# Squares, bonus input and k's scaling of a time-mixing stage on GpSimd, with other buffers and banks

## The reference

```python
w = -softplus(-(w0 + tanh(xw @ w1) @ w2)) - 0.5
decay = exp(-exp(w))
a = sigmoid(a0 + (xa @ a1) @ a2)
g = sigmoid(xg @ g1) @ g2
kk = heads(k * k_k)
kk = kk / maximum(sqrt(sum(kk * kk, -1)), 1e-12)
k = k * (1 + (a - 1) * k_a)
...
bonus = sum(rh * kh * r_k, -1) * vh
out = ((norm(y) + bonus) * g) @ w_o
```

## Time and profile before

| | |
|---|---|
| time, median of 3 runs | 3338.79 us (3338.55 to 3340.55) |
| profiled execution, its own time | 3345.62 us |
| span of that execution | 3343.8 us |
| TensorE matmul, weight load | 3082.7 us (92%), 2754.2 us (82%) |
| VectorE | 2405.0 us (72%) |
| ScalarE | 1660.4 us (50%) |
| GpSimd | 123.0 us (4%) |
| granted TensorE clock, mean | 0.933 of full |

### The profile page before, as it was taken

How to read it: one execution, slowest core, us unless ns; L and a number is a source line. 1 busy time by engine, 2 the same in 40 slices (tenths; PEclk the granted TensorE clock), 3 DMA queues, 4 the chain that set the end, 5 groups by cost and what they waited for, 6 DMA issues and landing times. The chain is left out here.

```text
span 3343.8 us, 58689 instructions
## 1 busy us (share of the span) xinstructions
PE 3082.7 (92%) x23865; PEld 2754.2 (82%) x23865; DVE 2405.0 (72%) x3656; ACT 1660.4 (50%) x2382; POOL 123.0 (4%) x178
## 2 busy tenths in 40 slices
PE   7679999899888899999988899999999998988899
PEld 6567778689877789898976899899789898878798
DVE  6569999688775468787577578786578788674555
ACT  4437777554552354544552444544554544442444
POOL 0010000000102000000000000000000001011000
PEclk8779999899999799999986899999999999998899
DMA  9347999667410267586430377674157586300442
GB/s 382 140 170 288 400 402 373 247 262 310 178 64 4 95 249 305 219 313 265 155 137 1 120 298 281 257 306 178 74 229 306 221 314 260 116 2 3 166 182 80
DMA packets 77519, 698.09 MB, mean 209 GB/s; under 512 B 8433, under 2 KB 12657, under 8 KB 55409
## 3 DMA queue, kind: packets, MB, share of 16 engines
q1 hardware_dynamic: 30928, 525.06, 39.8%
q10 hardware_dynamic: 42912, 157.31, 12.4%
q0 software_dynamic: 3456, 12.58, 1.0%
HBM read 690.72 MB, written 4.19 MB: 208 GB/s over the span
## 5 line engine op out<-in xcount | busy, mean ns | idle before, releaser
L1075 PE MATMUL banks<-u_split,w_split 128*128 128x512 f32 x2816 | 1014.7, 403 | 23.3 <-DVE u_split L1320 21.2
L1144 ACT ACTIVATE w_split<-ring 128x1024 fp32r<-128x1024 f32 x513 | 541.4, 1058 | 672.6 <-PE banks L1076 408.8
L1251 DVE TENSOR_TENSOR w_split<-ring,w_split 128x1024 fp32r<-128x1024 f32 x513 | 625.9, 1223 | 293.9 <-ACT w_split L1144 290.0
L1076 PE MATMUL banks<-u_split,w_split 128*128 128x256 f32 x2816 | 797.0, 283 | 0.0
L1075 PEld LDWEIGHTS banks<-u_split,w_split 128*128 128x128 f32 x2816 | 536.8, 191 | 159.3 <-issue 17.6
L1076 PEld LDWEIGHTS banks<-u_split,w_split 128*128 128x128 f32 x2816 | 539.6, 192 | 0.0
L1067 PE MATMUL banks<-h_split,w_split 128*128 128x256 f32 x1408 | 400.7, 285 | 7.5 <-DVE w_split L1251 7.5
L1068 PE MATMUL banks<-h_split,w_split 128*128 128x256 f32 x1408 | 400.4, 284 | 0.0
L1069 PE MATMUL banks<-h_split,w_split 128*128 128x256 f32 x1408 | 400.3, 284 | 0.0
L521 PE MATMUL banks<-bufs_split,ring_split 128*128 128x256 f32 x1376 | 397.3, 289 | 0.0
L585 DVE CUSTOM_DVE_ANT_0 bufs<-bufs 128x1024 f32<-128x1024 f32 x300 | 357.0, 1224 | 12.0 <-DVE w_split L1251 12.0
(11 more groups left out here) (497 smaller groups left out, 4872.4 us busy)
## 6 DMA issues: line engine op xcount, KB each, us to landing
ring<-stream SPq DMA_DIRECT2D x155, 3072.0 KB, 11.0
bufs<-ada ACTq DMA_DIRECT2D x296, 512.0 KB, 10.7
bufs<-ada POOLq DMA_DIRECT2D x23, 512.0 KB, 6.6
bufs<-ada SPq DMA_DIRECT2D x3, 2048.0 KB, 16.0
ring<-stream SPq DMA_DIRECT2D x2, 2688.0 KB, 9.0
bufs<-c_rows SPq DMA_DIRECT2D x9, 512.0 KB, 4.4
ring<-stream SPq DMA_DIRECT2D x1, 2704.0 KB, 13.1
ring<-stream SPq DMA_DIRECT2D x1, 2176.0 KB, 8.4
```

The source lines that it names most:

```text
L1075: pe.matmul(bank.rearrange("p (a t) -> p a t", a=2), w_high, u_split[:, k, :, :], start=(k == 0), stop=False, skip_group_check=True)
L1076: return pe.matmul(bank[:, 0:SEQ], w_low, u_split[:, k, 0, :], start=False, stop=(k == KC - 1), skip_group_check=True)
L1144: nc.scalar.activation(w_split[:, slot, 0, :], piece(j, b), ACT.Copy).then_inc(high.sem, 1)
L1251: e = nc.vector.tensor_tensor(w_split[:, slot, 1, :], piece(j, b), w_split[:, slot, 0, :].bitcast(F32), ALU.subtract)
```

## The change

The squares of kk, the bonus input, the scaling of k by its exponential and half of that of r move to GpSimd. The squares go to the buffer of `dx`, the bonus input to that of `g`. On TensorE the square sums come after the last down product, and both gate up products go into the halves of bank 6. On VectorE the clamp of the sums moves behind the third quarter, and the last two products change places. On ScalarE the first two gate copies move into the middle of the second exponentials, behind a wait for the bonus sums, because the copies write the buffer of the bonus input.

```diff
@@ -2757,7 +2757,8 @@
     flat = lambda x: x.rearrange("p c t -> p (c t)")
     by_chunk = lambda x: flat(x).rearrange("p (q t) -> p q t", t=P)
     two = lambda x, q: x[:, 2 * q:2 * q + 2, :]
-    kk, up_exp, down_exp, squares, bonus_in, bonus = h, x_w, dx, a, x_g, x_w
+    kk, up_exp, down_exp, squares, bonus_in, bonus = h, x_w, dx, dx, g, x_w
+    half = lambda x, q: flat(x)[:, q * KC // 2 * SEQ:(q + 1) * KC // 2 * SEQ]
     kc = lambda x: core.col(f"{x}{n}")
     narrow = core.narrow
     rate = -float(np.exp(-0.5))
@@ -2766,6 +2767,7 @@
                  "w_ready", "centered", "k_mixed", "r_exp", "k_exp", "normed", "mixed", "projected", "a_projected",
                  "evacuated", "a_evacuated", "g_evacuated", "up_done", "narrow_ready", "padded", "v_first_stored")
         sig = {x: core.event(x) for x in names}
+        sig["bonus_weighed"], sig["r_scaled"] = core.event("turned"), core.event("turned_sb")
 
         def wait(eng, name, count):
             eng.wait_ge(sig[name].sem, sig[name].at(count))
@@ -2786,8 +2788,27 @@
 
         @block.gpsimd
         def _(pool):
-            pool.memset(narrow[32:HEAD, 1, :], 0.0)
+            made(pool.memset(narrow[32:HEAD, 1, :], 0.0), "padded")
             made(pool.memset(narrow[HEAD:P, 1, :], 0.0), "padded")
+            wait(pool, "padded", 2)
+            wait(pool, "mixed", 1)
+            for q in range(4):
+                wait(pool, "raw_copied", q + 1)
+                made(pool.tensor_tensor(two(squares, q), two(kk, q), two(kk, q), ALU.mult), "squared")
+            wait(pool, "up_done", 2)
+            for c in range(KC):
+                last = pool.tensor_scalar(bonus_in[:, c, :], r[:, c, :], kc("r_k")[:, c:c + 1], None, ALU.mult)
+            made(last, "bonus_weighed")
+            wait(pool, "bonus_weighed", 1)
+            for q in range(4):
+                wait(pool, "k_mixed", q + 1)
+                made(pool.tensor_tensor(two(bonus_in, q), two(bonus_in, q), two(k, q), ALU.mult), "bonus_in")
+            wait(pool, "r_exp", 1)
+            made(pool.tensor_tensor(half(r, 1), half(r, 1), half(up_exp, 1), ALU.mult), "r_scaled")
+            wait(pool, "bonus_in", 4)
+            for q in range(2):
+                wait(pool, "k_exp", q + 1)
+                pool.tensor_tensor(half(k, q), half(k, q), half(down_exp, q), ALU.mult)
 
         @block.vector
         def _(dve):
@@ -2812,7 +2833,7 @@
                     last = dve.tensor_scalar(up_exp[:, c, :], a[:, c, :], -1.0, kc("k_a")[:, c:c + 1], ALU.add, ALU.mult)
                 link(last)
                 made(dve.scalar_tensor_tensor(two(k, q), two(up_exp, q), 1.0, two(k, q), ALU.add, ALU.mult), "k_mixed")
-                if q == 1:
+                if q == 2:
                     wait(dve, "square_sum", 1)
                     made(dve.tensor_scalar(values, core.psum[:, 7, 0:2 * RW_HEADS], 1e-24, None, ALU.max), "scaled")
             wait(dve, "w_ready", 4)
@@ -2822,26 +2843,21 @@
             made(dve.tensor_scalar(plus_mid, mid, rate, None, ALU.mult), "centered")
             wait(dve, "rooted", 1)
             made(dve.reciprocal(values, values), "inverse")
-            wait(dve, "k_mixed", 4)
-            wait(dve, "up_done", 4)
-            for c in range(KC):
-                last = dve.scalar_tensor_tensor(bonus_in[:, c, :], r[:, c, :], kc("r_k")[:, c:c + 1], k[:, c, :], ALU.mult, ALU.mult)
-            made(last, "bonus_in")
             for q in range(4):
                 wait(dve, "spread", q + 1)
                 made(dve.tensor_tensor(two(kk, q), two(kk, q), spread_bank(q), ALU.mult), "normed")
             wait(dve, "normed", 4)
             link(dve.tensor_tensor(flat(a), flat(a), flat(kk), ALU.mult))
             wait(dve, "r_exp", 1)
-            wait(dve, "bonus_in", 1)
-            dve.tensor_tensor(flat(r), flat(r), flat(up_exp), ALU.mult)
             dve.scalar_tensor_tensor(by_chunk(kk)[:, :, 1:], by_chunk(kk)[:, :, 1:], -1.0, by_chunk(up_exp)[:, :, 0:P - 1], ALU.mult, ALU.mult)
-            link(dve.scalar_tensor_tensor(by_chunk(kk)[:, :, 0], by_chunk(kk)[:, :, 0], -1.0, e_first, ALU.mult, ALU.mult))
-            wait(dve, "k_exp", 1)
-            dve.tensor_tensor(flat(k), flat(k), flat(down_exp), ALU.mult)
+            dve.scalar_tensor_tensor(by_chunk(kk)[:, :, 0], by_chunk(kk)[:, :, 0], -1.0, e_first, ALU.mult, ALU.mult)
+            wait(dve, "bonus_weighed", 1)
+            link(dve.tensor_tensor(half(r, 0), half(r, 0), half(up_exp, 0), ALU.mult))
+            wait(dve, "bonus_sums", 1)
+            wait(dve, "r_scaled", 1)
+            dve.tensor_tensor(flat(bonus), core.psum[:, 0:4, :].rearrange("p b t -> p (b t)"), flat(v), ALU.mult)
+            wait(dve, "k_exp", 2)
             dve.tensor_tensor(flat(a), flat(a), flat(down_exp), ALU.mult)
-            wait(dve, "bonus_sums", 1)
-            dve.tensor_tensor(flat(bonus), core.psum[:, 0:4, :].rearrange("p b t -> p (b t)"), flat(v), ALU.mult)
 
         @block.tensor
         def _(pe):
@@ -2871,10 +2887,6 @@
             for c in range(KC):
                 q = c // 2
                 if q == 3 and c % 2 == 0:
-                    for b in range(KC):
-                        wait(pe, "squared", b // 2 + 1)
-                        last = sums_by_token(core, pe, squares, b, 7, RW_HEADS)
-                    made(last, "square_sum")
                     wait(pe, "evacuated", 1)
                     wait(pe, "a_evacuated", 1)
                 last_w = pe.matmul(w_bank(q)[:, c % 2, :], w2[0:HEAD, c * P:(c + 1) * P], narrow[0:HEAD, 0, :], start=True, stop=True)
@@ -2884,13 +2896,15 @@
                     made(last_a, "a_projected")
             core.used(pe, (f"w2{n}", 0), last_w, sig["projected"])
             core.used(pe, (f"a2{n}", 0), last_a, sig["a_projected"])
+            for b in range(KC):
+                wait(pe, "squared", b // 2 + 1)
+                last = sums_by_token(core, pe, squares, b, 7, RW_HEADS)
+            made(last, "square_sum")
             wait(pe, "mixed", 1)
             for b in range(2):
                 key = (f"g1{n}", b)
                 m = core.place[key][2] // KC
-                if b:
-                    wait(pe, "scaled", 1)
-                core.project(pe, key, lambda q: x_g[:, q, :], core.psum[0:m, 6 + b, 0:SEQ], sig["up_done"], m=m)
+                core.project(pe, key, lambda q: x_g[:, q, :], core.psum[0:m, 6, b * SEQ:(b + 1) * SEQ], sig["up_done"], m=m)
             wait(pe, "evacuated", 4)
             wait(pe, "a_evacuated", 4)
             wait(pe, "inverse", 1)
@@ -2899,10 +2913,10 @@
                 if c % 2:
                     made(last, "spread")
             wait(pe, "narrow_ready", 4)
-            wait(pe, "padded", 1)
+            wait(pe, "padded", 2)
             g_down(0)
             g_down(1)
-            wait(pe, "bonus_in", 1)
+            wait(pe, "bonus_in", 4)
             wait(pe, "normed", 4)
             for c in range(KC):
                 last = pe.matmul(spread_bank(c // 2)[:, c % 2, :], core.const("heads"), bonus_in[:, c, :], start=True, stop=True)
@@ -2912,10 +2926,6 @@
 
         @block.scalar
         def _(act):
-            def square(q):
-                wait(act, "raw_copied", q + 1)
-                made(act.activation(two(squares, q), two(kk, q), ACT.Square), "squared")
-
             def two_sigmoids(out, q, source, name, done, bias):
                 wait(act, name, 2 * q + 2)
                 act.activation(out[:, 2 * q, :], source(q)[:, 0, :], ACT.Sigmoid, bias=bias[:, 2 * q:2 * q + 1])
@@ -2929,18 +2939,14 @@
             made(act.activation(narrow[0:HEAD, 0, :], core.psum[0:HEAD, 6, 0:SEQ], ACT.Tanh), "narrow_ready")
             made(act.activation(narrow[HEAD:P, 0, :], core.psum[HEAD:P, 6, 0:SEQ], ACT.Copy), "narrow_ready")
             for q in range(4):
-                square(q)
-            for q in range(4):
                 two_sigmoids(lw, q, w_bank, "projected", "evacuated", core.col(f"w0{n}"))
-                if q == 0:
-                    wait(act, "square_sum", 1)
                 two_sigmoids(a, q, a_bank, "a_projected", "a_evacuated", core.col(f"a0{n}"))
             wait(act, "scaled", 1)
             made(act.activation(values, values, ACT.Sqrt), "rooted")
             for b in range(2):
                 m = core.place[(f"g1{n}", b)][2] // KC
-                wait(act, "up_done", 3 + b)
-                made(act.activation(narrow[0:m, b, :], core.psum[0:m, 6 + b, 0:SEQ], ACT.Sigmoid), "narrow_ready")
+                wait(act, "up_done", 4)
+                made(act.activation(narrow[0:m, b, :], core.psum[0:m, 6, b * SEQ:(b + 1) * SEQ], ACT.Sigmoid), "narrow_ready")
             wait(act, "centered", 1)
             wait(act, "k_mixed", 4)
             act.activation(e_mid, mid, ACT.Exp, scale=rate)
@@ -2949,10 +2955,13 @@
             for p in range(16):
                 last = act.activation(by_chunk(up_exp)[:, p, :], by_chunk(lw)[:, p, :], ACT.Exp, scale=rate, bias=less_mid[:, p:p + 1])
```

(7 more changed lines are left out.)

## The result

| | before | after |
|---|---|---|
| time, median of 20 runs each on the same chip, us | 3338.67 (3332.91 to 3345.57) | 3346.28 (3341.48 to 3351.54) |
| ratio to before, 95% interval | 1 | 1.0021 (1.0014 to 1.0027) |
| span of the profiled execution, us | 3343.8 | 3347.5 |
| first and second pass of the stage, us | 43.0 and 43.4 | 46.3 and 47.1 |
| busy over the span: VectorE, ScalarE, GpSimd, us | 2405.0, 1660.4, 123.0 | 2419.3, 1655.7, 177.8 |

The change makes the kernel slower by 7.6 us; the forecast was 6.0 slower. A pass is counted here from VectorE's first instruction of the stage to its first of the next stage. In the one profiled execution of each kernel the two passes grow by 3.3 and 3.7 us, 7.0 together, but the spans differ by only 3.7: the rest of the kernel, which the change leaves alone, took 3.3 us less in that execution.

A forecast was written before the change was run, and what follows sets the result against it. It took TensorE as busy for most of the span and VectorE as setting the edited stage's end; +3.0 us a pass, +6.0 in all, added to the median 3338.8 gave 3344.8 us, range 3336 to 3353.

The forecast's parts named there:

- my signs of being wrong: Listed trace findings against the forecast, among them GpSimd scalings over 0.64 us and half clock granted after the spread.
- Turns between the engines: Edited stage: VectorE instructions with both inputs in SBUF and GpSimd's alternate, whole instruction by whole instruction; +3.0 us a pass.
- The step from rows 5 to the scans: A VectorE product stretched to 3.31 us from 1.23 beside GpSimd; the stage's scans were taken to wait likewise.
- rival B: VectorE's one-input scalings run free beside GpSimd: k scaling ends at 957.6, +0.9 us a pass, 3340.6; chance 0.13.
- the k scalings: Start of the pass on VectorE: turns with GpSimd's squares add 3 x 1.12 us, ending at 961.0 instead of 957.6.
- the tail: From the reciprocal at 978.2 to the pass's last product, taken as 997.9 against 994.9 before.
- GpSimd's scaling: Eight one-input scalings of 256 columns at 0.45 us each, between 0.36 and 0.64; each costs VectorE's loop 0.3.
- Gate products at no cost: Both in one bank on TensorE, ending near 974 to 975; costed at nothing because TensorE then waits for the reciprocal.
- rival A: TensorE's clock falls while it waits for the reciprocal: some 2.2 us more, +5.2 a pass, 3349.2; chance 0.19.
- ScalarE's wait for the bonus sums: After eight of sixteen second exponentials ScalarE stops until 989.1; that path ends about 997.3, VectorE's own chain at 998.1.
- A reading that was wrong: TensorE's square sums take 4.58 us because the squares stand in the buffer that the second sigmoids write.
- Rival C: No contention, scans stay at 0.34 us beside GpSimd: -2.6 to -5.0 us a pass, 3328.8 to 3333.6; chance 0.10.

The follow-up runs named there:

- the control: The changed kernel with the scans' ones copied elsewhere in SBUF and the narrow products in rotating banks: 3342.28 us, ratio 1.0001.
- the last two versions: Kernel before with half of k's last scaling on GpSimd; squares on ScalarE, sums between gate products: 3335.37 us, 0.9985; or squares on GpSimd: 3336.48 us, 0.9984.

## Why the forecast was right, and where it was not

The sign, the place and nearly the size came out: +7.6 us for +6.0. But that the size came out is luck: two errors cancel in it, turns taken too dear and a fall of the clock priced at nothing. Two of my signs of being wrong came true, GpSimd scalings over 0.64 us and the half clock behind the stand. Times into the first pass:

| | forecast | after |
|---|---|---|
| k scalings end | 8.9 | 7.83 |
| centring starts | 25.3 | 23.58 |
| reciprocal over | 26.1 | 25.45 |
| gate products end | 22 to 23 | 22.95 |
| spreading lasts | 3.7 | 5.31 |
| last VectorE product over | 45.8 | 46.03 |

**Turns between the engines: right, taken 1.1 to 1.5 us a pass too dear.** The step from rows 5 to the scans held: they stand beside GpSimd and run free with PSUM. That scalings take turns too, on which rival B turned, is in the trace: 4.54 us for 2.19. By the Trainium skill, "SBUF — State Buffer", section "Who interferes with whom", a tensor_scalar can enter a two-port mode and then contends with GpSimd. The 4.54 us agree; no row of before could show it. After the work that VectorE lost, the turns cost 1.9 and 1.5 us a pass by the control's records, and at most 1.7 by its timed runs, where I had 3.0. The mis-sized terms: the k scalings cost 2.35 us instead of 3.4 (the 16-column subtraction takes back some of that); and the tail from the reciprocal to the end takes 19.2 us at full clock, where I had 19.7.

**GpSimd's scaling: duration wrong, price right.** I took 0.45 us, with bounds of 0.36 and 0.64; it lasts 1.02. I charged duration less 0.15, that is 0.3; it holds VectorE for 0.24. "Duration less its start" nearly holds for the two-input products (beside the four bonus products of 1.08 us VectorE's instructions took 0.99 to 1.07 us longer; beside the squares three of its k scalings lost 0.78 each) and not for these. One error hid the other.

**Gate products at no cost: this is the step that failed.** They ended where I said, and TensorE did wait, 2.64 and 4.20 us. But the wait was not free: the clock fell in it, the spreading took 1.6 and 2.4 us more. That was rival A, at a chance of 0.19 and a price of 2.2; place and price were about right, though all of it is the spreading: the gate pairs behind it, which I had slow in part, keep 3.72 us in both passes. I had given it too little because full-width matmuls come right before the stand.

**ScalarE's wait for the bonus sums.** It was there, as the timeline of ScalarE after shows (two gate copies after 5.29 us of idle time), but I had VectorE's own chain coming out alike, and it was that chain that counted.

```profile
991.83 1.09 ACT L2936 ACTIVATE bufs<-banks 128x512 f32<-128x512 f32 x2 [5.29 <-PE banks L2922]
```

**A reading that was wrong.** The square sums do not take 4.58 us because of the buffer: with the squares elsewhere they still take 4.19. What the shared buffer makes is the sigmoids' wait for them.

**Rival C** is out: scans at 3.36 / 4 = 0.84 us beside the bonus products, not 0.34.

**What stays open.** How the 7.6 us divide. By the records of one execution 3.4 are turns and 3.6 the clock. By timed runs the turns are worth between nothing and 3.3, the clock and what else differs in TensorE's order the rest; no timed run takes the clock's fall alone. Nor is it settled when a stand costs the clock: it fell in stands of 2.64, 4.20 and 4.31 us and held through stands of 2.39, 2.56, 2.75 and 2.86. And most of what the last two versions gain has no place in the traces yet.

## What to carry to other kernels

Before moving work to an idle engine, look where the operands of the busy engine lie at that moment: here GpSimd took no time from VectorE only beside instructions with an input in PSUM. The two versions with work put there are 0.15% faster, of which the tail accounts for 1.5 us; beside VectorE instructions with all inputs in SBUF the same engine won nothing that the runs can tell, or lost. Then ask what the wait that is opened does to the engine that waits: here TensorE's stand made the matmuls behind it 1.6 to 2.4 us longer. And a hole in one engine's timeline is worth no more than the other engines' orders let through: here the gate products ended where the hole did.

## What was not expected of the hardware

- A GpSimd scaling by a per-partition column, 128x256, takes 0.92 to 1.12 us, nearly as much as a two-input product of twice the columns (1.08), yet holds VectorE for 0.24 on average.
- An instruction of 16 columns takes its turn like any other: 1.25 us instead of 0.18, and 2.33 in the control's tail, beside a GpSimd product of 1024 columns.
- Neither engine keeps the other off for long: beside three bonus products, VectorE's scans come in between, each waiting for one product (1384 and 1420 ns, then 393 and 393).
